# Delta rule on TensorE: where the modulation tiles and the old step's products stand between the levels of a triangular inverse

## The chip, the core and the metric

The kernel runs on one core of a Trainium2 chip. The metric is device time in microseconds (us), the median of three runs: 2932.6 us (2932.4 to 2933.28). A difference under about 0.2% (5.9 us) cannot be told from no change here.

A core has TensorE (matmuls, written PE in the rows, PEld for its weight loads), VectorE (DVE), ScalarE (ACT), GpSimd (POOL) and SyncE (SP, which here only issues DMAs). Each engine runs its own instructions in order and waits for the others through semaphores. Matmul results land in PSUM, which has 8 banks of 512 columns of float32.

## The reference, cut to what matters

The program is one block with a bidirectional gated delta rule and a mixture of experts, then two transformer layers. The change touches only the delta rule of the first block and the modulation product that is computed beside it:

```python
mod = silu(c) @ w_mod + b_mod          # [6 * 1024]; the second network has another of these
# per head (4), per direction (2), in chunks of 64 tokens; 256 context tokens, then 512
lmat = strict_lower((k * beta) @ k.T * decay)
tinv = inverse(eye + lmat)
u, w = tinv @ (v * beta), tinv @ (k * beta * exp(gc))
intra = q @ k.T * decay
def step(s, chunk):                    # in order over the chunks
    v_new = u_i - w_i @ s
    o     = qd_i @ s + a_i @ v_new
    s     = s * gl_i + kd_i.T @ v_new
```

Everything is float32.

## The kernel before, in words

**Tile steps.** The 768 tokens are six tiles of 128 tokens, each two chunks of 64. `delta_pe`, `delta_act` and `delta_dve` write out the programs of TensorE, ScalarE and VectorE for s = -1 to 5. In the round of s, the "new" tile s + 1 is prepared (its triangular inverse is built) while the "old" tile s goes through its two state updates n = 0 and n = 1. Tiles 0 and 1 are context and give no output; for tiles 2 to 5 `with_out` holds. Below, "step k" is the stretch that prepares tile k and ends with its `keys_pe` (line 974); it holds the updates of tile k - 1.

**The inverse.** The 64 by 64 triangle of each head and direction is inverted by block doubling. Level 0 is a mask. For levels l = 1 to 5 and directions d = 0 and 1, `first_pe` (line 947, 16 small products for each direction, bank `TB + d`) is masked by VectorE in `first_dve` (line 1168), `second_pe` (line 964, bank `UB + d`) takes that, and `second_dve` subtracts (line 1175) and transposes (line 1178), after which the next level's `first_pe` can start. Each level so goes twice from TensorE to VectorE and back. `keys_pe` follows level 5.

**The old tile's updates.** `value_pe(s, n)` (lines 984, 994, and 1005 for output) fills bank `VB`, ScalarE copies it (line 1091), `state_pe(s, n)` (lines 1015 and 1022) makes the state's increment and the output. On VectorE `decay_dve` (1187) scales the state, `state_dve` (1192) adds the increment, `out_dve` (1204 or 1207) takes the output, and `query_dve` (1162) scales queries for the tile being prepared.

**The modulation tiles.** `later` is a `RowModulation`: twenty tiles of 512 columns of the two modulation matrices (2 MB each). SyncE loads them into two slots (line 201); the load of tile n + 2 waits until the product of tile n is done. The product of a tile is 64 small matmuls (line 212: weights of one column, 128 moving columns), its row is copied and stored by ScalarE (lines 223 and 225). Before the change a tile stands in front of `second_pe` of direction 0, at levels 1 to 4 in steps 0 and 1 and at levels 2 to 4 in steps 2 to 5, and uses bank `TB`, which `first_pe` of the next level also uses.

**Around it.** Ahead of level 1 of step 0 four groups of transposes for another branch run (`cfturn_pe`, line 76), copied by ScalarE (line 1269). `cf_root_act` (lines 1279 and 1281, with two table loads) stands behind `keys_act` of step 0. When the twentieth tile's product is done, SyncE loads the two halves of `w_out`; `heads_pe` (line 369 there) waits for both. The mixture of experts begins behind a barrier that closes this part, at 576.8 us.

Of the kernel before, what the change touches and what calls it, by code (L numbers as in the profile page):

```python
# [17 lines left out]
NT = T // P  # L18
# [161 lines left out]
class RowModulation:  # L180
# [22 lines left out]
    def pe(self, bank):  # L203

        n, pe, depth, width = self.product.n, self.nc.tensor, len(self.slots), self.COLS // self.GROUPS
        w, cond = self.slots[n % depth], self.parts[n][1]
        pe.wait_ge(self.loaded[n % depth].sem, 16 * (n // depth + 1))
        if n >= 1:
            pe.wait_ge(self.copied.sem, n)
        for k in range(KD):  # L210
            for g in range(self.GROUPS):
                mm = pe.matmul(bank[32 * g:32 * g + 1, 0:width], cond[:, k:k + 1], w[:, k, g * width:(g + 1) * width],
                               start=k == 0, stop=k == KD - 1)
        mm.then_inc(self.product.sem, self.product.up())
# [70 lines left out]
def mixers(nc, X, x_in, c, ctx_in, c_ctx, w_mod, b_mod, g_mix, w_in, w_out, conv_w, a_log, dt_bias, norm_g,  # L285
           cf_w, cf_b, cf_ln_g, cf_ln_b, c_2, mod_w_2, mod_later, consts):
    pe_, act_, dve_, pool_ = nc.tensor, nc.scalar, nc.vector, nc.gpsimd
    with Scope(nc) as ctx:
# [242 lines left out]
        def later_levels(s):  # L531
            return (1, 2, 3, 4) if s < 2 else (2, 3, 4)
# [398 lines left out]
        def first_pe(s, l, d):  # L931

            if l == 1:
                pe_.wait_ge(lt_r.sem, s + 1)
                pe_.wait_ge(m_ev.sem, 2 * s + d + 1)
                if d == 0:
                    if with_out(s):
                        pe_.wait_ge(intra_r.sem, s - NCT + 1)
                    else:
                        pe_.wait_ge(r_relu.sem, 8 * (s + 1))  # L940
            else:
                pe_.wait_ge(up_ev[d].sem, (INV - 1) * s + l - 1)
            if d == 0:
                pe_.wait_ge(later.copied.sem, later.product.n)
            for h in range(4):
                for c in range(2):
                    mm = pe_.matmul(PS[rows(c), TB + d, sq64(0, h)], lt[rows(c), sq64(d, h)], m_of(s, d)[rows(c), sq64(0, h)], start=True, stop=True)
            mm.then_inc(t1_mm[d].sem, t1_mm[d].up())

        def second_pe(s, l, d):  # L950
# [7 lines left out]
            if d == 0 and l in later_levels(s):  # L958
                later.pe(PS[:, TB, :])
# [66 lines left out]
        def delta_pe():  # L1026
# [4 lines left out]
            for s in range(-1, NTA):  # L1031
# [3 lines left out]
                if s < 0:  # L1035
                    cfturn_pe()
                    pe_.wait_ge(cfturn.copied.sem, NT)
# [4 lines left out]
                if not new:  # L1042
                    pe_.wait_ge(cf_silu.sem, NT)
                    for k in (4, 5):
                        heads_turn_pe(k)
                if old:
# [4 lines left out]
                if new:  # L1051
                    for d in range(2):
                        first_pe(s + 1, 1, d)
                if old:
                    value_pe(s, 1)
                if new:
                    for d in range(2):
                        second_pe(s + 1, 1, d)
                    for d in range(2):
                        first_pe(s + 1, 2, d)  # L1060
                if old:
                    state_pe(s, 1)
                if new:
                    for d in range(2):
# [38 lines left out]
        def delta_act():  # L1103
            for s in range(-1, NTA):
# [5 lines left out]
                if old:  # L1110
                    value_act(s, 0)
                if s < 0:
                    cf_square_act()
                if not new:
# [4 lines left out]
                if new:  # L1119
                    for _ in later_levels(s + 1)[:-2]:  # L1120
                        later.act(PS[:, TB, :])
                    scaled_keys_act(s + 1, kg, egc, kg_r)
                    later.act(PS[:, TB, :])
                    scaled_keys_act(s + 1, kd[(s + 1) % 2], ekd, kd_r)
                    later.act(PS[:, TB, :])
# [3 lines left out]
                    if s < 0:  # L1129
                        cf_root_act()  # L1130
# [78 lines left out]
        def delta_dve():  # L1209
            dve_.wait_ge(ld_const.sem, 16)  # L1210
            dve_.memset(ST[:, :], 0.0).then_inc(s_zero.sem, s_zero.up())
            for s in range(-1, NTA):
# [9 lines left out]
                if old:  # L1222
                    state_dve(s, 0)
                    if with_out(s):
                        out_dve(s, 0)
                    if s < LAST:
                        decay_dve(s, 1)
                    else:
                        head_sums_dve((1, 2))
                if new:  # L1230
                    for d in range(2):
                        first_dve(s + 1, 1, d)
                    if with_out(s + 1):
                        query_dve(s + 1)
                    for d in range(2):
                        second_dve(s + 1, 1, d)
                    for d in range(2):
                        first_dve(s + 1, 2, d)
                if old:
                    if s < LAST:  # L1240
                        state_dve(s, 1)
                    if with_out(s):
                        out_dve(s, 1)
                if new:
                    for d in range(2):
                        second_dve(s + 1, 2, d)
                    for l in range(3, INV):
                        for d in range(2):
                            first_dve(s + 1, l, d)
                        for d in range(2):  # L1250
                            second_dve(s + 1, l, d)
                if 0 <= s < NT:
# [7 lines left out]
        def cfturn_pe():  # L1260
            pe_.wait_ge(cf_conv.sem, 4)
            pe_.wait_ge(z_ev.sem, NT)
            for t in range(NT):
# [3264 lines left out]
```

## Time and profile before

| | us |
|---|---|
| median of three runs | 2932.6 |
| the profiled execution | 2939.04 |
| its span, first to last instruction | 2937.2 |
| TensorE busy, of the span | 2702.5 |
| VectorE busy | 1341.7 |
| ScalarE busy | 672.8 |
| delta rule, steps 0 to 5 (270.3 to 502.4) | 232.1 |
| heads stage begins (line 369) | 515.5 |

The times of the parts are those of one profiled execution. "Busy" of TensorE counts a matmul from its start to a modelled end, so that small matmuls in a row overlap and their starts tell more than their sum. A row of the timeline merges instructions of one kind: start, length to the last end, and in brackets how long the engine had been idle and what ended that. The table of windows gives for each stretch the length and, for each engine, busy time and number of instructions; then TensorE's granted clock as a share of 2.4 GHz, the busy share of the DMA engines, and GB/s. "issue" is a wait that the profile puts down to no instruction: a load that had not landed, or instructions that had not come.

### The profile page before, as it was taken

To read this page: it belongs to the slowest core of one execution; us is meant where nothing else is said; L and a number is where in the kernel's file an instruction comes from. 1 tells how busy PE (TensorE), PEld (TensorE's weight loads), DVE (VectorE), ACT (ScalarE), POOL (GpSimd) and SP (SyncE) were. 2 spreads that over 40 slices of the span, in tenths; PEclk is the share of its full clock that TensorE was granted. 3 is DMA by queue.
4 is the path that set the end of the run, shared out by engine and by line. 5 is a ranking of instruction groups with operands and counts; after the bars stand their busy time and mean duration, and the time that the engine had idled before them with its cause. 6 is when DMAs were issued, how large, how long until landed. Compare 5 with 4: busy or idle time off the path is not lost.

```text
span 2937.2 us, 38706 instructions
## 1 busy us (share of the span) xinstructions
PE 2702.5 (92%) x15523; PEld 1743.2 (59%) x15523; DVE 1341.7 (46%) x2785; ACT 672.8 (23%) x1531; POOL 246.7 (8%) x369
## 2 busy tenths in 40 slices
PE   5999888899888898959999999999999999999998
PEld 3545777464333333424466568888844665688887
DVE  2635566452111111164845567754448455433443
ACT  2134233111111111122332433310022324333000
POOL 0000000001111111111110011100012100000000
PEclk9999999999999999979999999999999999999999
DMA  6103545167999999652101035532230110222320
GB/s 237 58 30 127 191 174 189 33 258 303 416 406 411 405 401 407 233 238 110 44 30 66 32 129 208 212 123 86 83 113 26 48 58 29 71 92 91 113 86 29
DMA packets 146807, 469.76 MB, mean 160 GB/s; under 512 B 15389, under 2 KB 28731, under 8 KB 120519
## 3 DMA queue, kind: packets, MB, share of 16 engines
q1 hardware_dynamic: 126468, 416.19, 37.1%
q0 software_dynamic: 18912, 50.36, 4.6%
q8 instruction: 123, 2.02, 0.3%
q10 hardware_dynamic: 1251, 0.77, 0.1%
q14 instruction: 53, 0.43, 0.0%
HBM read 460.90 MB, written 26.28 MB: 166 GB/s over the span
## 4 chain that ended last, share of the span: by engine, by line
PE 48%; DVE 5%; ACT 1%; issue 1%; POOL 0%; DVEq 0%; ACTq 0%; POOLq 0%
PE ps_l L2636 41%; PE ps_l L3158 2%; PE ps_l L76 1%; PE ps_l L3366 1%; DVE pT_notsel_l L3135 1%; PE ps_l L3824 1%; DVE small_l L3133 1%; DVE small_l L3484 1%; PE ps_l L3194 1%; DVE pT_notsel_l L3125 0%; PE ps_l L3240 0%; PE ps_l L159 0%; PE ps_l L3104 0%; PE ps_l L2820 0%; PE ps_l L3465 0%
## 5 line engine op out<-in xcount | busy, mean ns | idle before, releaser
L2129 PE MATMUL ps_m<-w_m,gatheredT_m 128*64 128x512 f32 (+1 forms) x816 | 305.3, 637 | 48.2 <-issue 46.4
L2636 PE MATMUL ps_l<-ring_l,hT_l 128*128 128x256 f32 (+3 forms) x960 | 313.2, 469 | 0.0
L2636 PE MATMUL ps_l<-early,hT_l 128*128 128x512 f32 (+1 forms) x576 | 260.6, 591 | 6.6 <-ACT hT_l L2827 3.0
L2636 PEld LDWEIGHTS ps_l<-ring_l,hT_l 128*128 128x128 f32 x960 | 174.6, 190 | 104.1 <-issue 83.2
L2129 PEld LDWEIGHTS ps_m<-w_m,gatheredT_m 128*64 128x64 f32 (+1 forms) x816 | 107.9, 164 | 180.6 <-issue 178.8
L2247 DVE TENSOR_TENSOR silu_m<-silu_m,ps_m 128x256 f32<-128x256 f32 x42 | 17.7, 421 | 360.1 <-ACT silu_m L2199 359.9
L2636 PE MATMUL ps_l<-hT_l,ring_l 128*128 128x256 f32 (+1 forms) x704 | 179.9, 405 | 0.9 <-ACT arena_l L3715 0.9
L369 PE MATMUL ps_a<-arena_a,ring_a 128*128 128x512 f32 (+2 forms) x496 | 169.9, 519 | 0.9 <-DVE arena_a L516 0.9
L2636 PE MATMUL ps_l<-ring_l,arena_l 128*128 128x256 f32 x768 | 169.1, 379 | 0.7 <-ACT arena_l L168 0.7
L2636 PEld LDWEIGHTS ps_l<-early,hT_l 128*128 128x128 f32 x576 | 104.9, 193 | 106.5 <-issue 96.4
L2636 PEld LDWEIGHTS ps_l<-ring_l,arena_l 128*128 128x128 f32 x768 | 145.8, 190 | 21.4 <-ACT arena_l L168 1.6
L2636 PEld LDWEIGHTS ps_l<-hT_l,ring_l 128*128 128x128 f32 x704 | 134.7, 193 | 30.1 <-issue 11.1
L2153 PE MATMUL ps_m<-w_m,aT_m 128*64 128x512 f32 (+1 forms) x408 | 145.3, 597 | 1.1 <-DVE aT_m L2257 1.1
L369 PEld LDWEIGHTS ps_a<-arena_a,ring_a 128*128 128x128 f32 (+1 forms) x496 | 87.3, 182 | 83.8 <-issue 77.9
L2129 PE MATMUL ps_m<-hT_m,gatheredT_m 128*64 128x512 f32 (+1 forms) x240 | 119.2, 655 | 16.2 <-issue 16.2
L2636 PE MATMUL ps_l<-consts_l,work_l 128*128 128x256 f32 x512 | 122.1, 381 | 2.5 <-DVE consts_l L3754 2.5
L2199 ACT ACTIVATE silu_m<-ps_m 128x256 f32<-128x256 f32 x42 | 16.1, 383 | 438.5 <-PE ps_m L2129 438.5
L2636 PEld LDWEIGHTS ps_l<-consts_l,work_l 128*128 128x128 f32 x512 | 96.3, 190 | 24.5 <-issue 11.9
L2636 PE MATMUL ps_l<-hT_l,early 128*128 128x256 f32 x384 | 89.0, 380 | 0.9 <-ACT ropework_l L3715 0.9
L130 DVE SCALAR_TENSOR_TENSOR gla_l<-pT_notsel_l,small_l,gla_l 128x256 f32<-128x256 f32 x168 | 81.5, 485 | 6.0
L2253 DVE COPY rows_io_m<-ps_m 128x512 f32<-128x512 f32 x42 | 29.0, 691 | 120.4 <-PE ps_m L2153 120.4
L2153 PEld LDWEIGHTS ps_m<-w_m,aT_m 128*64 128x64 f32 (+1 forms) x408 | 47.9, 153 | 55.4 <-issue 53.3
(620 smaller groups left out, 4209.1 us busy)
## 6 DMA issues: line engine op xcount, KB each, us to landing
w_m<-in_exp_w_gate SPq DMA_DIRECT2D x51, 1024.0 KB
w_m<-in_exp_w_up SPq DMA_DIRECT2D x51, 1024.0 KB
w_m<-in_exp_w_down SPq DMA_DIRECT2D x51, 1024.0 KB, 12.7
ring_l<-in_mlp_w SPq DMA_DIRECT2D x22, 2048.0 KB, 7.8
ring_a<-in_mod_w SPq DMA_DIRECT2D x12, 2048.0 KB, 9.3
pT_notsel_l<-in_mod_w POOLq DMA_DIRECT2D x24, 1024.0 KB, 5.6
early<-in_mlp_w SPq DMA_DIRECT2D x10, 2048.0 KB, 7.9
ring_a<-in_w_mod SPq DMA_DIRECT2D x9, 2048.0 KB, 9.0
```

Of the source, the lines that this page charges most:

```text
L76: mm = self.nc.tensor.transpose(self.banks[n % len(self.banks)][0:src.shape[1], bank_cols], src, self.ident[0:src.shape[0], 0:src.shape[0]])
L130: dve.scalar_tensor_tensor(out, w[:, k, :], cond[:, k:k + 1], out, ALU.mult, ALU.add).then_inc(signal.sem, signal.up())
L369: mm = pe_.matmul(out, lhsT, rhs, start=start, stop=stop)
L2129: mm = pe_.matmul(PS[h * rows:(h + 1) * rows, 2, :], hg[s % 2][:, k, h * rows:(h + 1) * rows], gu_w[w][:, k, :, :], start=k == 0, stop=k = ...
L2153: mm = pe_.matmul(PS[h * rows:(h + 1) * rows, 4 + half, :], AT[:, at:at + rows], dn_w[w][:, k, half * 512:(half + 1) * 512], start=k == 0, ...
L2636: mm = pe_.matmul(out, lhsT, rhs, start=start, stop=stop, **group)
L3133: dve_.max(top, nb[:, i, 0:s]).then_inc(own_v.sem, own_v.up())
L3135: dve_.match_replace(nb[:, i, 0:s], top, nb[:, i, 0:s], TAKEN).then_inc(own_v.sem, own_v.up())
L3158: mm = pe_.matmul(PS[:, 6, h * 64:(h + 1) * 64], src[:, j, h, :], proj[:, j, c:c + 64], start=j == 0, stop=j == i)
L3194: pe_.matmul(PS[:, h, 0:s], TB[o:o + 64, h // 2, i * P:(i + 1) * P], TB[o:o + 64, 6, 0:s], start=True, stop=True).then_inc(at_mm.sem, at_m ...
L3366: mm = pe_.matmul(PS[:, 2 * (n % 2) + h % 2, 0:P], a_, b_, start=True, stop=True, tile_position=(32 * h, 0))
L3484: dve_.tensor_reduce(mx[:, b:b + 2], PS[:, b:b + 2, 0:s], AX.X, ALU.max).then_inc(own_v.sem, own_v.up())
```

## The change

- The product of a modulation tile is cut in two halves of 32 matmuls (`pe(bank, half)`), and stands behind `second_pe` of a level instead of in front of it. Steps 2 to 4 have a tile at levels 3, 4 and 5, step 5 at levels 2, 3 and 4. Step 1 has one ahead of the first state product and at levels 3, 4 and 5. Step 0 has one between the transposes, one spread over levels 1 and 2, one over levels 3 and 4, and one at level 5. It stays at twenty tiles.
- Its bank is `OB` for tiles 0 and 1 and `VB` after them; `first_pe` no longer waits for the copy of a tile, `value_pe` does.
- `value_pe(s, 1)` stands behind the second products of level 1 (it stood in front of them), `state_pe(s, 1)` behind those of level 2.
- VectorE follows: the first output copy stands between the two passes of level 1, `decay_dve` behind level 1, `state_dve` behind level 2, the second output copy behind level 3, `query_dve` behind level 4. In the last round its order stays.
- ScalarE: `cf_root_act` moves from behind `keys_act` of step 0 to directly behind `cf_square_act`; the tile copies follow their tiles.

```diff
-    def pe(self, bank):
+    def pe(self, bank, half):
...
-        pe.wait_ge(self.loaded[n % depth].sem, 16 * (n // depth + 1))
-        if n >= 1:
-            pe.wait_ge(self.copied.sem, n)
-        for k in range(KD):
+        if half == 0:
+            pe.wait_ge(self.loaded[n % depth].sem, 16 * (n // depth + 1))
+            if n >= 1:
+                pe.wait_ge(self.copied.sem, n)
+        for k in range(half * KD // 2, (half + 1) * KD // 2):
...
-        def later_levels(s):
-            return (1, 2, 3, 4) if s < 2 else (2, 3, 4)
+        BEFORE_STATE = 0
+        def later_halves(s):
+            if s == 0:
+                return {BEFORE_STATE: (0, 1), 1: (0,), 2: (1,), 3: (0,), 4: (1,), 5: (0, 1)}
+            if s == 1:
+                return {BEFORE_STATE: (0, 1), 3: (0, 1), 4: (0, 1), 5: (0, 1)}
+            return {l: (0, 1) for l in ((3, 4, 5) if s < NTA - 1 else (2, 3, 4))}
...
+        def later_bank(s):
+            return PS[:, OB if s < NCT else VB, :]
+        def later_pe(s, at):
+            for half in later_halves(s).get(at, ()):
+                later.pe(later_bank(s), half)
         def value_pe(s, n):
             if vn_mm.n:
                 pe_.wait_ge(vn_ev.sem, vn_mm.n)
+            pe_.wait_ge(later.copied.sem, later.product.n)
...
                 if new:
-                    for d in range(2):
-                        second_pe(s + 1, 2, d)
-                    for l in range(3, INV):
+                    for l in range(1, INV):
                         for d in range(2):
                             first_pe(s + 1, l, d)
                         for d in range(2):
                             second_pe(s + 1, l, d)
+                        if old and l == 1:
+                            value_pe(s, 1)
+                        if old and l == 2:
+                            state_pe(s, 1)
+                        later_pe(s + 1, l)
                     keys_pe(s + 1)
...
                 if s < 0:
                     cf_square_act()
+                    cf_root_act()
...
                 if new:
-                    for l in range(3, INV):
+                    for l in range(1, INV):
                         for d in range(2):
                             first_dve(s + 1, l, d)
+                        if old and l == 1 and with_out(s):
+                            out_dve(s, 0)
                         for d in range(2):
                             second_dve(s + 1, l, d)
+                        if old and l == 1:
+                            decay_dve(s, 1)
+                        if old and l == 2:
+                            state_dve(s, 1)
+                        if old and l == 3 and with_out(s):
+                            out_dve(s, 1)
+                        if l == 4 and with_out(s + 1):
+                            query_dve(s + 1)
```

TensorE, before, from level 1 to the first product of level 3 in steps 4 and 5 (L947 is the first product, L964 the second, L984 to L1005 the value product, L1015 and L1022 the state product, L212 a modulation tile):

```order
L947 MATMUL ps_a<-arena_a 64x64 x16
L984 MATMUL ps_a<-tok_a,arena_a 64x128 x8
L994 MATMUL ps_a<-states_a,arena_a 64x128 x8
L1005 MATMUL ps_a<-states_a,arena_a 64x128 x8
L964 MATMUL ps_a<-arena_a 64x64 x16
L947 MATMUL ps_a<-arena_a 64x64 x16
L1015 MATMUL ps_a<-arena_a 128x128 x8
L1022 MATMUL ps_a<-arena_a 64x128 x8
L212 MATMUL ps_a<-ring_a,cond_a 1x128 x32
L964 MATMUL ps_a<-arena_a 64x64 x16
L947 MATMUL ps_a<-arena_a 64x64 x16
```

The same stretch of TensorE in the changed kernel, up to the first tile (L957 is now the first product, L972 the second, L1000 to L1021 the value, L1031 and L1038 the state product, L213 a tile):

```order
L957 MATMUL ps_a<-arena_a 64x64 x16
L972 MATMUL ps_a<-arena_a 64x64 x16
L1000 MATMUL ps_a<-tok_a,arena_a 64x128 x8
L1010 MATMUL ps_a<-states_a,arena_a 64x128 x8
L1021 MATMUL ps_a<-states_a,arena_a 64x128 x8
L957 MATMUL ps_a<-arena_a 64x64 x16
L972 MATMUL ps_a<-arena_a 64x64 x16
L1031 MATMUL ps_a<-arena_a 128x128 x8
L1038 MATMUL ps_a<-arena_a 64x128 x8
L957 MATMUL ps_a<-arena_a 64x64 x16
L972 MATMUL ps_a<-arena_a 64x64 x16
L213 MATMUL ps_a<-ring_a,cond_a 1x128 x32
```

The value, state and tile products stood between a first and a second product; now they stand between a second product and the next level's first, and the first tile has moved from level 2 to level 3.

TensorE at the start of step 0 in the changed kernel, from the transposes (L76) to level 2; before, both groups of transposes stood together and a whole tile of x32 stood between L947 and L964 at each of levels 1 to 4:

```order
L76 MATMUL ps_a<-consts_a,cf_o_a 128x128 x8
L213 MATMUL ps_a<-ring_a,cond_a 1x128 x32
L76 MATMUL ps_a<-consts_a,cf_o_a 128x128 x8
L957 MATMUL ps_a<-arena_a 64x64 x16
L972 MATMUL ps_a<-arena_a 64x64 x16
L213 MATMUL ps_a<-ring_a,cond_a 1x128 x16
L957 MATMUL ps_a<-arena_a 64x64 x16
L972 MATMUL ps_a<-arena_a 64x64 x16
L213 MATMUL ps_a<-ring_a,cond_a 1x128 x16
```

A tile has gone ahead of level 1, and each of levels 1 and 2 has half a tile behind its second product.

VectorE of the changed kernel in step 3, from the first output copy on (L1220 output copy, L1188 subtraction, L1191 transpose, L1200 scaling of the state, L1181 mask of a first product, L1205 state sum):

```order
L1220 COPY cf_o_a<-ps_a 64x512 x2
L1188 TENSOR_TENSOR arena_a<-arena_a,ps_a 128x256
L1191 STREAM_TRANSPOSE arena_a<-arena_a 128x256
L1188 TENSOR_TENSOR arena_a<-arena_a,ps_a 128x256
L1191 STREAM_TRANSPOSE arena_a<-arena_a 128x256
L1200 TENSOR_TENSOR arena_a<-states_a,chunk_decay_a 128x1024
L1181 TENSOR_TENSOR arena_a<-ps_a,consts_a 128x256 x2
L1188 TENSOR_TENSOR arena_a<-arena_a,ps_a 128x256
L1191 STREAM_TRANSPOSE arena_a<-arena_a 128x256
L1188 TENSOR_TENSOR arena_a<-arena_a,ps_a 128x256
L1191 STREAM_TRANSPOSE arena_a<-arena_a 128x256
L1205 TENSOR_TENSOR states_a<-arena_a,ps_a 128x1024
```

The long operations (output, scaling, state sum) stood ahead of a level's masks or between them and the subtractions; now each stands behind the work of a level, the output copy alone stands in front of subtractions.

## Rows read from the trace of the kernel before

**Rows 1.** Windows, one per tile step (0 to 5); columns as explained above
```profile
270.32:305.70 35.38, 26.85 (x657) 21.97 (x657) 15.28 (x36) 15.61 (x47) 0.00 (x0) 0.90 0.77 272
305.70:347.09 41.39, 32.38 (x768) 28.11 (x769) 19.58 (x39) 13.35 (x36) 0.00 (x0) 0.92 0.59 206
347.09:382.59 35.50, 31.17 (x752) 27.20 (x753) 23.88 (x46) 11.40 (x33) 0.00 (x0) 1.00 0.49 175
382.59:424.46 41.87, 35.62 (x816) 31.91 (x817) 26.71 (x50) 11.40 (x33) 0.00 (x0) 0.96 0.50 179
424.46:462.98 38.52, 34.69 (x817) 30.72 (x817) 26.70 (x50) 11.40 (x33) 0.00 (x0) 1.00 0.38 137
462.98:502.38 39.40, 34.74 (x817) 30.80 (x817) 26.67 (x50) 14.87 (x38) 0.00 (x0) 1.00 0.34 117
```

**Rows 2.** Timeline, TensorE, step 4: start us, us, engine line operation, idle
```profile
436.40 1.10 PE L947 MATMUL ps_a<-arena_a 64*64 64x64 f32 x32
437.33 1.04 PE L984 MATMUL ps_a<-tok_a,arena_a 64*64 64x128 f32 x16
...
440.20 1.15 PE L964 MATMUL ps_a<-arena_a 64*64 64x64 f32 x32
...
443.88 1.16 PE L1015 MATMUL ps_a<-arena_a 64*128 64x128 f32 x16
...
445.99 1.93 PE L212 MATMUL ps_a<-ring_a,cond_a 128*1 128x128 f32 x64
447.85 1.15 PE L964 MATMUL ps_a<-arena_a 64*64 64x64 f32 x32
...
459.69 1.47 PE L947 MATMUL ps_a<-arena_a 64*64 64x64 f32 x32 [0.54 <-DVE arena_a L1178]
460.98 1.38 PE L964 MATMUL ps_a<-arena_a 64*64 64x64 f32 x32
462.98 2.00 PE L974 MATMUL ps_a<-arena_a 64*128 64x64 f32 x32 [0.62 <-DVE arena_a L1175]
```

**Rows 3.** Groups by line, VectorE, 270 to 516 us: busy, mean ns, idle
```profile
L1168 DVE TENSOR_TENSOR arena_a<-ps_a,consts_a 128x256 f32<-128x256 f32 x60 | 25.0, 423 | 13.6 <-PE ps_a L947 13.4
L1175 DVE TENSOR_TENSOR arena_a<-arena_a,ps_a 128x256 f32<-128x256 f32 x60 | 24.3, 405 | 47.2 <-PE ps_a L964 47.0
L1178 DVE STREAM_TRANSPOSE arena_a<-arena_a 128x256 f32<-128x256 f32 x48 | 21.4, 445 | 1.7
L1187 DVE TENSOR_TENSOR arena_a<-states_a,chunk_decay_a 128x1024 f32<-128x1024 f32 x11 | 13.4, 1221 | 0.2
```

**Rows 4.** DMA issues, one tile load each, issued at 448.0, 406.1 and 377.7 us
```profile
ring_a<-in_mod_w SPq DMA_DIRECT2D x1, 2048.0 KB, 7.8
...
ring_a<-in_mod_w SPq DMA_DIRECT2D x1, 2048.0 KB, 9.1
...
ring_a<-in_mod_w SPq DMA_DIRECT2D x1, 2048.0 KB, 11.7
```

**Rows 5.** Timeline, ScalarE, step 1
```profile
308.78 1.28 ACT L1279 ACT_TABLE_LOAD   x1
```

**Rows 6.** Timeline, TensorE, first product of step 0, and state product in step 1
```profile
278.80 1.97 PE L947 MATMUL ps_a<-arena_a 64*64 64x64 f32 x32 [1.73 <-ACT cf_o_a L1269]
...
314.63 1.55 PE L1015 MATMUL ps_a<-squares_a,arena_a 64*128 64x128 f32 x16 [2.72 <-ACT squares_a L1091]
```

**Rows 7.** Windows: three stretches of TensorE's clock
```profile
277.90:284.70 6.80, 5.90 (x108) 4.47 (x109) 1.88 (x6) 3.21 (x9) 0.00 (x0) 0.51 0.01 4
315.40:322.20 6.80, 5.41 (x66) 4.81 (x66) 5.29 (x9) 0.00 (x0) 0.00 (x0) 0.51 0.00 0
338.60:342.00 3.40, 1.74 (x65) 1.60 (x64) 0.42 (x1) 0.27 (x1) 0.00 (x0) 1.00 1.03 379
```

**Rows 8.** Timeline, TensorE, last modulation tile of step 1
```profile
340.26 1.93 PE L212 MATMUL ps_a<-ring_a,cond_a 128*1 128x128 f32 x64 [1.66 <-issue]
```

**Rows 9.** DMA issues, the second load of w_out, issued at 498 us
```profile
ring_a<-in_w_out SPq DMA_DIRECT2D x1, 2048.0 KB, 13.5
```

More of the change, by code:

```diff
@@ L213, in pe @@
                                start=k == 0, stop=k == KD - 1)
-        mm.then_inc(self.product.sem, self.product.up())
+        if half == 1:
+            mm.then_inc(self.product.sem, self.product.up())
     def act(self, bank):
@@ L529, in mixers, with later_copies @@
                            [SQ[:, 1088 + r * P:1088 + (r + 1) * P] for r in range(2)], mod_later)
-        def later_levels(s):
-            return (1, 2, 3, 4) if s < 2 else (2, 3, 4)
+        BEFORE_STATE = 0
[5 more added lines that the diff above has]
+            return {l: (0, 1) for l in ((3, 4, 5) if s < NTA - 1 else (2, 3, 4))}
+        def later_copies(s):
+            return sum(halves.count(1) for at, halves in later_halves(s).items() if at != BEFORE_STATE)
         p_mm, p_ev, cb_zero, conv, conv_silu = sig("p_mm"), sig("p_ev"), sig("cb_zero"), sig("conv"), sig("conv_silu")
@@ L1035, in delta_pe @@
                 if s < 0:
-                    cfturn_pe()
+                    cfturn_pe((0, 1))
+                    later_pe(s + 1, BEFORE_STATE)
+                    cfturn_pe((2, 3))
                     pe_.wait_ge(cfturn.copied.sem, NT)
@@ L1045, in delta_pe @@
                         heads_turn_pe(k)
+                if old and new:
+                    later_pe(s + 1, BEFORE_STATE)
                 if old:
@@ L1111, in delta_act @@
                     value_act(s, 0)
+                if new and BEFORE_STATE in later_halves(s + 1):
+                    later.act(later_bank(s + 1))
                 if s < 0:
                     cf_square_act()
+                    cf_root_act()
                 if not new:
@@ L1119, in delta_act @@
                 if new:
-                    for _ in later_levels(s + 1)[:-2]:
-                        later.act(PS[:, TB, :])
                     scaled_keys_act(s + 1, kg, egc, kg_r)
-                    later.act(PS[:, TB, :])
+                    later.act(later_bank(s + 1))
                     scaled_keys_act(s + 1, kd[(s + 1) % 2], ekd, kd_r)
-                    later.act(PS[:, TB, :])
+                    for _ in range(later_copies(s + 1) - 1):
+                        later.act(later_bank(s + 1))
                     if s == LAST - 1:
@@ L1258, in mixers, with cfturn_pe @@
         mu, vr = S[:, 448:452], S[:, 452:456]
-        def cfturn_pe():
+        def cfturn_pe(tiles_):
             pe_.wait_ge(cf_conv.sem, 4)
             pe_.wait_ge(z_ev.sem, NT)
-            for t in range(NT):
+            for t in tiles_:
                 cfturn.pe([(cc[:, cch, t * P:(t + 1) * P], slice(cch * P, (cch + 1) * P)) for cch in range(4)])
```

42 lines of the change are left out of this document (4 added, 38 removed).

## The prediction

> **What bounds the kernel now.** I read the stretch in which the change works, 270 to 502 us of a 2937 us span, first by windows of one tile step each. TensorE is busy 32 to 36 of about 40 us, VectorE 20 to 27, ScalarE 11 to 16 [rows 1]. The reader is to see that no engine is full: the steps are a chain that goes back and forth between TensorE and VectorE, and what counts is who stands in whose way. The timeline of step 4, a step with little disturbance, shows it. Level 5 has no tile: its first product starts at 459.69, its second at 460.98, `keys_pe` at 462.98. Half a microsecond ahead of the first and 0.62 us ahead of `keys_pe` TensorE is idle and waits for VectorE; at level 2 a tile (445.99 to 447.85, 1.86 us) stands ahead of the second product [rows 2]. By groups, VectorE needs 0.42 us for a mask, 0.41 for a subtraction, 0.45 for a transpose [rows 3] and waits 47 us in all for second products, since the tile holds them up. So before the change a tile covers only the short mask; the longer stretch, subtraction and transpose, is paid in idle time, and so is the tile.
>
> The second limit is the load. Each tile is 2 MB in one of two slots, and the slot of the third tile of a step is free only when the first is used up. Such a load takes 7.8 us with nothing in front of it, 9.1 in another step, 11.7 queued behind another [rows 4].
>
> **One level.** At level 5 today first and second product together take 2.60 us (1.29 to the second product's start, 1.3 for it) [rows 2], of which 0.3 is the wait of direction 1 for its transpose. Behind a tile or an old product both transposes are done and the two directions run without a gap, so I put the pair at 2.35 us (2.3 if nothing waits). With a whole tile a level then takes 2.35 + 1.86 = 4.2 us, with half a tile 3.3. VectorE's subtraction, transpose and again both, about 1.7 us by [rows 3], lie beside the tile. Before, a level with a tile took 1.1 + 1.86 + 1.1 and 0.54 idle, with 0.3 of transposes between the directions: 4.9 us.
>
> **Step 4, part by part.** `keys_pe` to the first product of level 1 is 436.40 - 424.46 = 11.94 us and is not changed [rows 1, 2]. From there, counted from 0: level 1 until 2.35; the value product 440.20 - 437.33 = 2.87, until 5.22; level 2, where the state's scaling of 1.22 us [rows 3] stands ahead of the masks and costs 0.2, until 7.77; the state product 445.99 - 443.88 = 2.11, until 9.88; level 3 until 12.23, tile until 14.09; level 4 with 0.2 for the output copy in front of the masks, 16.64, tile until 18.50; level 5 until 20.85. There the third tile is not ready. Its slot came free at 14.09, the load is issued 0.13 us later and takes 8.5 us (my value between 7.8 and 9.1, the middle): 22.7. With the tile, 24.6. The step takes 36.5 us instead of 38.52, a gain of 2.0 (2.7 with 7.8, 1.4 with 9.1). The wait of 1.9 us is new: before, the two levels between the tiles covered the load almost to the point.
>
> **The other steps, in the same way.** Step 5 has its tiles at levels 2 to 4 and the same wait at level 4: 37.1 instead of 39.40, gain 2.3. Step 3 is built as step 4 but took 41.87, 3.35 more than step 4 with the same instructions [rows 1]; it comes to 36.5, gain 5.4. Step 2 has shorter value and state products: 34.2 instead of 35.50, gain 1.3. Step 1: before, two table loads of 1.28 us each with their operations stand in ScalarE's order ahead of the copy that the state product needs (308.78) [rows 5], and TensorE is idle 2.72 us, until 314.63 [rows 6]. With these two behind the squares in step 0, where ScalarE has slack, `keys_pe`, setup and value product take 6.0 us, the tile that now stands there 1.9, beside ScalarE's chain, the state product 1.1: the first level begins at 9.1 instead of 11.9. Two levels without a tile, three with one, a value and a state product and the wait of about 1.9 us for the load give 33.0 instead of 41.39, gain 8.4. Step 0: the first product of level 1 stays at 278.80, since ScalarE's copies of the transposes release it [rows 6]. Four levels of 3.3 and a copy that holds one tile back by 0.35 are 13.5, level 5 with its tile 4.2: 296.5 instead of 305.70, gain 9.2. But in this stretch the clock was at 1.2 GHz from 277.9 to 284.7 (granted 0.51) [rows 7]; TensorE was idle ahead of it, and the tile between the transposes now fills part of that. If the clock falls all the same, half of what TensorE does in the stretch comes back, 5.90 / 2 = 2.9 us. I take 7.8, between 6.3 and 9.2. The stretch after 315.4, also at 1.2 GHz [rows 7], followed the 2.72 us of idle time, which goes; at worst 2.7 us come back.
>
> The sum is 7.8 + 8.4 + 1.3 + 5.4 + 2.0 + 2.3 = 27.2 us. Step 3's 3.35 us and 0.9 of step 5 over step 4 are stalls of the instruction or load supply that nothing in the change removes; I let half of them return, 2.1. That leaves 25.1 us. The added waits: the third tile delays `keys_pe` (priced above); `value_pe` waits for a tile's copy, 0.3 us on ScalarE, under the 1.9 us of `keys_pe`: nothing, at most 0.4 a step if that cover were gone. The tiles' new banks are free where they stand: nothing. SyncE's queue holds only the loads.
>
> Four more changes between a tile's array shape (128*1) and the level's (64*64) come from the halves of step 0; the tile's 64 matmuls and the second product behind them run on at 1.86 us without a gap [rows 2], so I price them at 0. The Trainium skill, TensorEngine Tiling (Array Packing), section Tiling Modes, says that a change of the tiling mode drains the array. By it each of the four would cost about one matmul's length, an estimate of 1 us in all; the row speaks for nothing.
>
> The profiled execution took 2939.04 us, 6.4 more than the median of 2932.6; the gain is taken off the median, where it is the same 0.9%. 2932.6 - 25.1 = 2907.5, rounded to 2907. What follows the barrier cannot give it back, because the experts' loads are issued only behind it.
>
> **The rivals.**
> 1. The waits for the third tile let the clock fall. Five steps get a wait of 1.9 us in a stretch of small matmuls. If each is followed by 6.8 us at half speed as in [rows 7], 5 x 2.9 = 14.5 us come back: 2922. For it: the two falls of [rows 7] followed idle TensorE. Against it: step 1 had a wait of 1.66 us for a load [rows 8], and the window around it shows a clock of 1.00 [rows 7]. The Trainium skill, TensorE: Matmul & The Clock Gate, section Loop structure matters more than you think, calls a DMA wait between groups of matmuls what makes the array go cold; by that rule the time would be this one.
> 2. The loads land early and the clock stays up: 0.7 us a step more, 1.4 in step 0, no stalls back (2.1), levels of 2.3: 2907.5 - 8 = 2899. For it: 7.8 has been seen with an idle queue [rows 4].
> 3. Slower. The loads of the third tiles, on which five steps now hang, land late. Each us beyond 8.5 costs 5 us and a little at step 0. To lose the 25.1 us they must take 8.5 + 25.1 / 5.5 = 13.1 us, and about 14.1 to be visibly slower (2939). The most seen in a ring load with one ahead is 11.7 [rows 4], the second load of `w_out` took 13.5 [rows 9]; but after the change the third tile's load has nothing ahead of it. 2939 and more.
> 4. It doesn't do what it says, because the heads stage waits for `w_out`: the second load is issued 0.5 us behind the last tile and takes 13.5 [rows 9], landing 14.1 behind it. The heads stage now begins about 16 us behind the last tile (level 5, `keys_pe`, two updates), before 18. The cover shrinks to 2 us; it would have to be gone by 20 us more for no change.
>
> **How the numbers follow.** Forecast with stalls and one or two short falls of the clock, 2901 to 2914: 0.62. Rival 1 whole or in part, 2914 to 2926: 0.17. Rival 2, below 2901: 0.14. No visible change (2927 to 2938; under 0.2%, 5.9 us, this measurement tells nothing): 0.04, rivals 1 and 4 together. Rival 3: 0.03. The range goes from 2898 to 2919: it holds the forecast, most of rival 2 and the lower half of rival 1. Faster 0.93, same 0.04, slower 0.03.
>
> **What would show it.** Steps of 36 to 37 us in 3 to 5 and 33 in step 1 (starts of `keys_pe`); a tile right behind each second product and no idle time ahead of levels 3 to 5; VectorE's wait for second products well under 47 us; at level 5 (4 in step 5) idle TensorE ahead of the tile, 1.2 to 2.5 us, ended by the load; step 0 ended by 296 to 300. The prediction is wrong if that wait is over 4 us, if the clock falls after each of them, or if the masks wait behind the moved state work by more than 1 us a level.

## The result: 0.54% faster, two thirds of the forecast gain

| | before | after |
|---|---|---|
| time, median of 20 runs each, us | 2936.34 (2932.34 to 2943.61) | 2918.62 (2908.21 to 2935.25) |
| ratio of the times | 1 | 0.9946, interval 0.9932 to 0.9959 |
| profiled execution, us | 2939.04 | 2926.64 |
| its span, us | 2937.2 | 2924.8 |
| stage: first setup product to the heads stage, us | 245.17 | 227.61 |
| of it steps 0 to 5, us | 232.1 | 214.5 |

The ratio is a gain of 15.9 us, the medians differ by 17.7, and the stage is 17.6 shorter; I had forecast 25.1 for it. The time lies at the upper edge of the range, 11.6 us above the forecast; 3.7 of these come from the starting point, since the kernel before has a median of 2936.34 over twenty executions where it had 2932.6 over three. The whole times scatter by several microseconds from one execution to the next (2908 to 2935 after the change). What lies behind the stage took 2421.7 us in the profiled execution before and 2429.0 after, 2418 to 2432 in the experiments below that can be compared; why is open. So I compare stages, and use whole times as a check.

The windows of one tile step each, of the kernel after (start to end us, length, busy us of TensorE, its weight loads, VectorE, ScalarE, GpSimd, granted clock, DMA share, GB/s), answer to [rows 1]:

```profile
268.22:296.98 28.76, 23.71 (x658) 20.20 (x657) 16.28 (x36) 18.10 (x50) 0.00 (x0) 1.00 0.77 268
296.98:335.88 38.90, 33.22 (x772) 29.05 (x769) 21.20 (x41) 10.49 (x32) 0.00 (x0) 0.88 0.65 230
335.88:369.65 33.77, 30.48 (x756) 27.38 (x752) 23.58 (x45) 11.30 (x33) 0.00 (x0) 0.98 0.47 165
369.65:407.03 37.38, 34.24 (x821) 30.69 (x817) 26.54 (x49) 11.29 (x33) 0.00 (x0) 0.98 0.54 194
407.03:445.09 38.06, 35.25 (x821) 31.65 (x817) 26.54 (x49) 11.29 (x33) 0.00 (x0) 0.95 0.48 170
445.09:482.72 37.63, 34.43 (x820) 31.04 (x817) 23.71 (x46) 13.58 (x37) 0.00 (x0) 0.99 0.40 134
```

The engines do the same work in less time, and the clock is no better than before: step 1 is at 0.88 where it was at 0.92, step 4 at 0.95 where it was at 1.00. Step 4 in TensorE's timeline (start us, us, engine, line, operation, idle before and who ended it) answers to [rows 2]:

```profile
431.28 1.93 PE L213 MATMUL ps_a<-ring_a,cond_a 128*1 128x128 f32 x64
433.14 1.15 PE L957 MATMUL ps_a<-arena_a 64*64 64x64 f32 x32
434.44 1.15 PE L972 MATMUL ps_a<-arena_a 64*64 64x64 f32 x32 [0.15 <-DVE arena_a L1181]
435.52 1.93 PE L213 MATMUL ps_a<-ring_a,cond_a 128*1 128x128 f32 x64
437.38 1.15 PE L957 MATMUL ps_a<-arena_a 64*64 64x64 f32 x32
438.59 1.15 PE L972 MATMUL ps_a<-arena_a 64*64 64x64 f32 x32
442.14 3.02 PE L213 MATMUL ps_a<-ring_a,cond_a 128*1 128x128 f32 x64 [2.40 <-DMA ring_a<-in_mod_w]
```

The reader is to see three things. Tiles and products stand with no gap over 0.15 us: a level with a tile takes 435.52 - 431.28 = 4.24 us (4.9 before). The one new wait stands where it was expected, ahead of the third tile, and it is 2.40 us instead of the assumed 1.9. And the tile behind that wait takes 3.02 us instead of 1.93: its clock fell. Windows of such stretches (same columns), which answer to [rows 7]:

```profile
299.50:306.30 6.80, 6.80 (x96) 6.45 (x96) 0.27 (x1) 3.40 (x10) 0.00 (x0) 0.50 0.77 288
402.00:405.40 3.40, 1.07 (x40) 0.98 (x44) 3.04 (x5) 0.00 (x0) 0.00 (x0) 0.98 1.03 352
405.40:408.80 3.40, 3.40 (x50) 2.71 (x44) 0.00 (x0) 0.28 (x1) 0.00 (x0) 0.52 0.92 314
442.90:446.30 3.40, 3.40 (x56) 2.60 (x50) 0.35 (x1) 0.28 (x1) 0.00 (x0) 0.51 0.93 339
```

With one more of 3.4 us from 333.7, TensorE works at 1.2 GHz for 17.0 us in all, as long as before (6.8 from 278.0, 6.8 from 315.5, 3.4 from 421.3). The window ahead of 405.40 shows what went before: 1.07 us of work in 3.40, since the third tile waited 2.73 us.

TensorE's waits by line, 268 to 496 us (us in total, times, longest), sum this up:

```profile
PE ps_a L213 <- DMA ring_a<-in_mod_w: 9.0, 4, 2.7
PE ps_a L213 <- DMA ring_a<-in_w_mod: 2.8, 1, 2.8
...
PE ps_a L972 <- issue: 1.6, 1, 1.6
PE ps_a L982 <- issue: 1.5, 1, 1.5
PE ps_a L957 <- issue: 0.9, 1, 0.9
```

The five waits for loads cost 11.8 us (2.75, 1.72, 2.73, 2.40, 2.19 in steps 1 to 5). "Issue" is idle time for which no engine and no load is named; three of these stand in steps 0 and 1:

```profile
283.33 0.91 PE L972 MATMUL ps_a<-arena_a 64*64 64x64 f32 x23 [1.62 <-issue]
...
293.08 0.91 PE L957 MATMUL ps_a<-arena_a 64*64 64x64 f32 x23 [0.88 <-issue]
...
299.09 2.55 PE L982 MATMUL ps_a<-arena_a 64*128 64x64 f32 x24 [1.45 <-issue]
```

They stand in the middle of a group of 32 matmuls (9 and then 23, 8 and then 24), where no matmul waits for a semaphore: TensorE lacks its next instructions. The trace shows these arriving, as packets of 16 KB on a DMA queue called "instruction" (39 of them from 268 to 510 us). In front of each stall such a packet ends, and TensorE goes on 1.3 to 1.6 us later:

| packet starts, us | ends | TensorE goes on | between |
|---|---|---|---|
| 280.88 | 281.99 | 283.33 | 1.34 |
| 290.50 | 291.53 | 293.08 | 1.55 |
| 296.70 | 297.77 | 299.09 | 1.32 |

It is so for all 45 stalls in the middle of a group in this run and the seven experiments that keep the new order (1.22 to 1.67 us). The trace doesn't say which engine a packet is for; but one comes every 6 us or so, and by chance about one stall in thirteen would fit. Behind the last of the three comes the fall of 6.8 us, which is why step 1 takes 38.90.

VectorE's wait for second products, by groups (busy, mean ns, idle), answers to [rows 3]:

```profile
L1188 DVE TENSOR_TENSOR arena_a<-arena_a,ps_a 128x256 f32<-128x256 f32 x60 | 24.4, 406 | 11.9 <-PE ps_a L972 11.5
```

It fell from 47.2 to 11.9 us, while the operation still takes 0.41 us: the reordering did what it was to do.

### The profile page after: what moved, and what is told of

It is laid out like the page before. It is cut to its first block, busy times and chain, and to the rows that moved or that the text cites. A ratio compares the mean times of both kernels' runs of the same rounds, so it can differ in the third digit from the quotient of the medians.

```text
span 2924.8 us, 38689 instructions
## 1 busy us (share of the span) xinstructions
PE 2700.2 (92%) x15523; PEld 1741.1 (60%) x15523; DVE 1341.0 (46%) x2785; ACT 672.9 (23%) x1531; POOL 247.3 (8%) x369
## 4 chain that ended last, share of the span: by engine, by line
PE 46%; DVE 6%; ACT 1%; issue 1%; SPq 0%; POOL 0%; DMA 0%; DVEq 0%; ACTq 0%; POOLq 0%
PE ps_l L2641 40%; PE ps_l L3163 2%; DVE pT_notsel_l L3140 1%; DVE small_l L3138 1%; PE ps_l L76 1%; PE ps_l L3371 1%; DVE pT_notsel_l L3130 1%; PE ps_l L3829 1%; DVE small_l L3489 1%; PE ps_l L3199 0%; PE ps_l L3245 0%; PE ps_l L159 0%; PE ps_l L3470 0%; DVE work_l L3503 0%; PE ps_l L3378 0%
## 5 line engine op out<-in xcount | busy, mean ns | idle before, releaser
L2252 DVE TENSOR_TENSOR silu_m<-silu_m,ps_m 128x256 f32<-128x256 f32 x42 | 17.7, 421 | 368.1 <-ACT silu_m L2204 367.9
L2641 PEld LDWEIGHTS ps_l<-hT_l,ring_l 128*128 128x128 f32 x704 | 134.7, 193 | 30.1 <-issue 11.1
L2641 PEld LDWEIGHTS ps_l<-consts_l,work_l 128*128 128x128 f32 x512 | 96.3, 190 | 24.5 <-issue 11.9
```

The lines of the kernel that those rows point to most:

```text
L2641: mm = pe_.matmul(out, lhsT, rhs, start=start, stop=stop, **group)
```

## The experiments

All edits are to the changed kernel unless said otherwise. A stage is that of the profiled execution of the run named; the stages of two executions of the same kernel differed by 1.7 us, which is the measure for small differences.

**The changed kernel once more.** No edit.

> The changed kernel once more, beside the others. Stage time means: from the first setup product of step 0 to the heads stage; before 245.2 us, changed 227.6 us in the traces at hand. Theory A (the stage gains 17.6 us, the rest of the program only scatters): stage 225 to 230, whole time 15 to 20 us below before. Theory B (the parts behind the stage give some of it back, as 7 us in the one trace): stage the same, whole time only 10 to 13 us below before.

Measured: 0.9936 (0.9921 to 0.9952), 18.8 us of the whole time, stage 225.9 us, as theory A has it. The load waits are the same in kind (2.70, 1.55, 2.71, 2.07, 2.11, together 11.1), and so is the half-speed time, 17.0 us, but not its place: 3.4 us from 279.8, 10.2 from 402.7, 3.4 from 477.8. Two of the three issue stalls return at the same matmul as before, to the instruction:

```profile
294.71 0.91 PE L957 MATMUL ps_a<-arena_a 64*64 64x64 f32 x23 [0.88 <-issue]
...
300.72 1.55 PE L982 MATMUL ps_a<-arena_a 64*128 64x64 f32 x24 [1.45 <-issue]
```

Here no fall of the clock follows the second, and step 1 takes 35.3 us. The third, of 1.62 us, is missing: the fall from 279.8 had held TensorE up ahead of it, and the packet, which ends at 283.75, came almost in time. Two small ones are new (0.31 and 0.28 us). So the load waits and most of the stalls are a property of the program; whether a fall follows one of them is not, and a fall can take a stall away.

**Half of each load.**

```
-        eng.dma_start(self.slots[r], self.parts[n][0])...
+        eng.dma_start(self.slots[r][:, 0:KD // 2, :], self.parts[n][0][:, 0:KD // 2, :])...
```

It leaves out half of each modulation tile's load. The modulation values are then others, what lies behind the stage takes some 100 us longer (I suppose since the experts get other tokens; not shown), and the whole time (2994.58 us) can't be compared; the stage can.

> Loads only the first 1 MB of each 2 MB modulation tile (the product then uses old data in the other half; leaves out half of the load). Theory A (the wait for the third tile of a step, 2.2 to 2.8 us in five steps, the falls of the clock behind it and the stalls of the instruction supply, 4 us in steps 0 and 1, all come from the load): stage 227.6 - 12 - 2 - 2 = about 212, no idle ahead of a tile. Theory B (the wait matters, but clock and stalls are of their own): stage 215 to 216. Theory C (a new wait takes its place): stage over 220.

Measured: stage 204.2 us, under the 212 of theory A, because more clock came back than the 2 us put down for it. Windows of steps 0, 1 and 5:

```profile
270.11:295.96 25.85, 23.30 (x657) 20.00 (x656) 16.28 (x36) 17.98 (x50) 0.00 (x0) 1.00 0.50 161
295.96:327.10 31.14, 29.03 (x772) 25.62 (x769) 19.47 (x40) 10.49 (x32) 0.00 (x0) 1.00 0.43 138
...
426.07:461.19 35.12, 33.90 (x820) 30.55 (x817) 25.42 (x48) 13.59 (x37) 0.00 (x0) 1.00 0.26 82
```

The clock is at 1.00 throughout, no tile waits for a load, and two issue stalls are left (0.63 and 0.23). With the loads at half their size all three losses go together: load waits, falls of the clock and most of the stalls. The stall that is left at the end of step 0 stands at the same matmul as the one of 1.45 us, and its packet starts 1.00 us ahead of `keys_pe` instead of 0.28. The packet of the 1.62 us stall tells more: it starts 12.66 us into the stage, in the second execution 12.70, with half loads 9.54, each time as the weights' transfers run out (the DMA share falls from about 1 to under 0.1 there), while TensorE was at its 270th, 232nd and 176th matmul of the stage. So it hung on the weights rather than on how far TensorE had got. This is what the chain of the new order takes with nothing in its way, and the base of the account below.

**Tiles spread so that the third load has time.**

```
             if s == 1:
-                return {BEFORE_STATE: (0, 1), 3: (0, 1), 4: (0, 1), 5: (0, 1)}
-            return {l: (0, 1) for l in ((3, 4, 5) if s < NTA - 1 else (2, 3, 4))}
+                return {BEFORE_STATE: (0, 1), 2: (0, 1), 3: (0,), 4: (1,), 5: (0, 1)}
+            return {2: (0, 1), 3: (0,), 4: (1,), 5: (0, 1)}
```

> Steps 1 to 5 have their tiles at level 2 (whole), level 3 (first half), level 4 (second half), level 5 (whole), so that the slot of the last tile comes free 9 us ahead of its use. Theory A (the load wait is what was mis-sized and can be covered by order alone): no wait over 0.5 us ahead of the last tile, steps 2 to 5 at 34 to 35 us, stage 216 to 218, with w_out landing about 1 us late for the heads stage. Theory B (the load wait is replaced by idle time at the levels with half a tile): stage 222 or more.

Measured: 0.9931 (0.9916 to 0.9947), stage 227.2 us, theory B. No load wait is left, and yet the stage is as long as after the change. TensorE's waits say why:

```profile
PE ps_a L982 <- issue: 6.3, 4, 2.2
...
PE ps_a L957 <- issue: 3.5, 3, 1.7
PE ps_a L1010 <- ACT arena_a L1108: 2.4, 1, 2.4
PE ps_a L957 <- DVE arena_a L1161: 1.8, 1, 1.8
PE ps_a L972 <- issue: 1.6, 1, 1.6
```

The issue stalls rise from 4 to 11.6 us, and the clock is down for 10.2 us (6.8 from 334.3, 3.4 from 484.5). Masks hold second products up for 6.0 us (2.6 in the changed kernel). The last tile at level 5 of step 5 also puts its copy into ScalarE's way, ahead of the copy of the keys (L1108), and the value product on the states (L1010) waits 2.38 us for that: from the end of step 5 to the heads stage it takes 16.8 us instead of 13.1. Spreading moves the loss, it doesn't remove it.

**Only the tiles moved; the old step's products back where they were.** In `delta_pe` value and state products of direction 1 stand again between first and second product of levels 1 and 2, and `delta_dve` has its order of before.

```
-                        for d in range(2):
-                            second_pe(s + 1, l, d)
                         if old and l == 1:
                             value_pe(s, 1)
                         if old and l == 2:
                             state_pe(s, 1)
+                        for d in range(2):
+                            second_pe(s + 1, l, d)
...
```

> Undoes one part of the changed kernel: the old step's value and state products and VectorE's order stand as before the change, the tiles stay behind the second products. Theory A (both moves pay; levels 1 and 2 then pay about 1.1 and 0.5 us of idle time): stage 234 to 236. Theory B (the tile placement does it all): stage 228.

Measured: 0.9993 (0.9979 to 1.0007), stage 235.0 us, within theory A, 10.2 us of it at half speed. The first products of levels 2 and 3 wait for VectorE's transpose again, nine times, 10.4 us in all (us in total, times, longest; then two of them in step 3's timeline):

```profile
PE ps_a L957 <- DVE arena_a L1191: 10.4, 9, 1.7
```
```profile
385.32 1.47 PE L957 MATMUL ps_a<-arena_a 64*64 64x64 f32 x32 [1.13 <-DVE arena_a L1191]
...
391.52 1.47 PE L957 MATMUL ps_a<-arena_a 64*64 64x64 f32 x32 [1.69 <-DVE arena_a L1191]
```

**Only the products moved; the tiles back ahead of the second products.** In `second_pe`, for d == 0 and the levels of before (`first_pe` of direction 0 then waits for a tile's copy again):

```
+            if d == 0 and l in ((1, 2, 3, 4) if s < 2 else (2, 3, 4)):
+                for half in range(2):
+                    later.pe(PS[:, TB, :], half)
```

> Undoes the other part of the changed kernel: the tiles stand in front of the second products as before the change, the value and state products, VectorE's order and the root stay as changed. Stage time (before 245.2, changed 226 to 228). Theory A (levels with a tile pay 0.5 us of idle time and the late transpose again, and the tile's load has two levels and a tile to land in, as before): stage 236 to 240, tile waits as before the change (under 1.7 us). Theory B (without the new waits for the load the old place is as good): stage 228 to 231.

Measured: 0.9982 (0.9969 to 0.9994), stage 238.9 us, 20.5 us of it at half speed (6.8 from 277.1, 3.4 from 314.7, 10.2 from 413.7), and within theory A. The longest wait that can be for a load is 1.35 us. TensorE's waits:

```profile
PE ps_a L959 <- DVE arena_a L1190: 7.5, 14, 0.5
...
PE ps_a L213 <- DVE arena_a L1180: 3.6, 5, 1.1
PE ps_a L959 <- issue: 3.2, 4, 1.4
```

The stage gains 10.2 us from the tiles alone and 6.3 from the products alone, 16.5 together, against 17.6 and 19.3 for both. But the clock was at half speed for 10.2 us in the one execution and 20.5 in the other, against 17.0; with half of the difference counted back, the gains are 6.8 and 8.0, 14.8 together. So these are two parts of similar size that give most of the whole; that the raw numbers add up so well is in part luck. In whole time each alone gives 2 and 5 us, where the change gives 15.9.

**The roots back in step 1.** `cf_root_act()` again behind `keys_act(s + 1)`.

```
-                    cf_root_act()
...
+                    if s < 0:
+                        cf_root_act()      # behind keys_act
```

> The changed kernel with ScalarE's root and its two table loads again behind the keys' copy of step 0. Theory A (they held the state product of step 1 back by 2.7 us): step 1 longer by 2 to 3 us, stage 229 to 230. Theory B (the modulation tile that now stands there covers them): under 1 us.

Measured: 0.9949 (0.9930 to 0.9968), stage 228.3 us. Step 1 takes 40.35 us against 38.90, both with the fall of 6.8 us from 299.5. The 1.5 us is between the two expectations and not above what two executions differ by; its visible part is a wait of 0.91 us ahead of a first product at 312.08, with no instruction packet near it. This part of the change is worth little at most.

**A third slot for the tiles.** A part of the array of `cf_o`, free once the squares are taken (the first load into it waits for that), and the arrays of the gates' bias become a third slot, so that a load can start one tile's product sooner (n - 2 products done instead of n - 1).

```
-        if n >= len(self.slots):
-            eng.wait_ge(self.product.sem, n - len(self.slots) + 1)
+        if n == 2 or n > 3:
+            eng.wait_ge(self.product.sem, 1 if n == 2 else n - 2)
...
+                           + [[part(CFO, 4 * T, 4 * 512, a=4), part(GBT, 0, 4 * 512, a=4)]],
```

> The changed kernel with a third slot for the tiles' loads, in two pieces of memory that are free in this stage; every tile is loaded in full. Theory A (the load, not the order, holds the stage back: with half the load it took 204.2): no wait for a tile's load, no fall of the clock behind one; stage 204 plus the 4 to 6 us of stalls in the instruction supply that the loads cause, 208 to 212; whole time 15 us below the changed kernel, about 2903. Theory B (as in the spread order: what the load wait took, stalls of the instructions and clock falls take instead): stage 222 or more. Theory C (w_out lands late for the heads stage): tail over 13.1 us.

Measured: 2906.21 us (2902.90 to 2917.34), ratio 0.9899 (0.9879 to 0.9919), stage 215.7 us, 3.7 us over theory A and far under B. It beats both kernels: its interval doesn't meet that of the change (0.9932 to 0.9959). Windows of its steps 0, 1 and 5:

```profile
269.95:300.50 30.55, 23.98 (x658) 20.16 (x657) 16.29 (x36) 18.06 (x50) 0.00 (x0) 1.00 0.93 325
300.50:334.21 33.71, 30.50 (x772) 27.03 (x768) 19.47 (x40) 10.49 (x32) 0.00 (x0) 0.95 0.62 216
...
437.99:472.55 34.56, 33.55 (x820) 30.33 (x817) 25.43 (x48) 13.57 (x37) 0.00 (x0) 1.00 0.36 126
```

No load wait, one fall of 3.4 us (from 304.4), and step 5 is 34.6 us as with half loads (35.1). Step 0, where the loads now stand closer (325 GB/s against 268), became 1.8 us longer: what is left is issue stalls, 9.4 us in eight of them, of which the largest groups are

```profile
PE ps_a L995 <- issue: 3.0, 3, 1.7
PE ps_a L225 <- issue: 2.8, 2, 1.4
```

(L995 is the first product of `keys_pe` there, L225 the tile's).

**The same third slot in the kernel before.** The same edit.

> The kernel before the change with the same third slot. Theory A (before the change the order, not the load, was the limit; the load cost it 1.1 and 1.7 us and some stalls): stage 239 to 243. Theory B (the load was the limit already): stage under 230.

Measured: 0.9986 (0.9974 to 0.9997), stage 243.2 us, as theory A has it but for 0.2 us. The half-speed time is 17.0 us as before. So the third slot is worth 2.0 us in the old order and 10 to 12 in the new one; before, as the prediction had it, the levels between the tiles covered the load almost to the point.

**Work in the place of the wait.** Ahead of the last tile of steps 1 to 5, 64 matmuls whose result nothing reads:

```
+        def filler_pe(s):
+            pe_.wait_ge(later.copied.sem, later.product.n)
+            for _ in range(2): ...
+                pe_.matmul(later_bank(s)[rows(c), sq64(d, h)], kk, kk, start=True, stop=True)
```

> The changed kernel with 64 more small products (2.2 us, of constant keys, into the bank that the tile then overwrites) ahead of the last tile of steps 1 to 5, where TensorE otherwise waits 1.7 to 2.8 us for that tile's load. They change no result and take the place of the wait. Theory A (the falls of the clock come from the idle time of that wait, and each us of a fall costs half a us): no fall behind a load wait, one or none in steps 0 and 1, stage 227.6 - 4 to 6 = 221 to 224 although TensorE does more. Theory B (the falls don't hang on the wait): falls as before, stage 226 to 231.

Measured: 0.9946 (0.9931 to 0.9962), stage 235.0 us, longer than either theory has it. The load waits shrink to 0.6 us and half-speed time to 6.8 us. But the issue stalls grow from 3 or 4 to 15.5 us, and both falls that are left follow one of them, not a load (timeline, then windows around 414.8):

```profile
407.54 1.50 PE L997 MATMUL ps_a<-kT_qT_a 128*64 128x64 f32 x43 [1.27 <-issue]
...
414.00 0.99 PE L982 MATMUL ps_a<-arena_a 64*128 64x64 f32 x12 [1.84 <-issue]
```
```profile
411.40:414.80 3.40, 1.56 (x26) 1.42 (x24) 0.00 (x0) 0.00 (x0) 0.00 (x0) 0.98 0.94 286
414.80:418.20 3.40, 3.40 (x62) 3.17 (x62) 0.00 (x0) 2.29 (x8) 0.00 (x0) 0.52 1.01 379
```

So a fall can follow idle time that no load ended. The added work took the place of the load waits, about 11 us for 11 us; beyond that it brought 11.6 us more of stalls and saved only 5.1 at the clock.

## Why the prediction was right and wrong

The direction and the mechanism were right; the gain was forecast at 25.1 us and was 17.6. The stage with half loads gives the base for an account by terms:

| term of the stage | forecast, us | measured, us | off by |
|---|---|---|---|
| chain of the new order, nothing in its way | 207.1 | 204.2 | -2.9 |
| waits for third tiles | 9.5 | 11.8 | +2.3 |
| half-speed clock (half of its time) | 1.4 | 8.5 | +7.1 |
| issue stalls | 2.1 | 3.1 | +1.0 |
| sum | 220.1 | 227.6 | +7.5 |

The forecast of the chain is 245.2 - 25.1 less the other three terms; the measured stalls are 3.95 less the 0.86 that stand with half loads too; 17.0 us at half speed are counted as 8.5. The same account holds for the second execution: 204.2 + 11.1 + 8.5 + 2.1 = 225.9, as measured. For the third slot it gives 214.4 of 215.7.

- **Levels.** 3.3 us with half a tile and 4.2 with a whole one: measured 287.44 - 284.17 = 3.27 (from one half's start to the next in step 0) and 4.24. Right; the chain as a whole was even 2.9 us shorter.
- **Masks behind the moved state work.** 0.15 us at level 4 of step 4, under the 0.2 allowed; in steps 1 and 2 three waits of 0.65 us for masks, 2.6 us in the whole stage. Far under the 1 us a level named. Right.
- **Halves of step 0 at no cost.** The rows of step 0 run on without a gap:

```profile
286.37 1.15 PE L972 MATMUL ps_a<-arena_a 64*64 64x64 f32 x32
287.44 1.05 PE L213 MATMUL ps_a<-ring_a,cond_a 128*1 128x128 f32 x32
288.43 1.15 PE L957 MATMUL ps_a<-arena_a 64*64 64x64 f32 x32
```

  A half takes 0.99 us from start to start, half of a whole tile 0.93; four such halves cost 0.2 us. The Trainium skill, TensorEngine Tiling (Array Packing), section Tiling Modes, has the array drained at such a change; if it is, less than 0.1 us of it shows here.
- **Waits for the third tile.** 1.9 us assumed, 2.36 in the mean. The load issued at 433.27 lands 8.8 us later instead of 8.5, and the next one behind it 10.3 later. The price of one load was about right, and the place as well. No wait was over the 4 us named.
- **The clock.** This is the step that failed: the term for the clock, put at 1.4 us, measured 8.5. The prediction let one fall return at half weight ("I take 7.8, between 6.3 and 9.2") and took the one after 315.4 as gone. A third one it did not see: step 3's 3.35 us [rows 1, clock 0.96] were put down to stalls, but the trace of before has 3.4 us at half speed from 421.1 there, beside stalls of 0.63 and 1.38. The falls did leave the places that they had, 278.0, 315.5 and 421.3, and came at new ones: 17.0 us at half speed before, 17.0 after, 17.0 once more in the second execution. That the three sums are equal is no rule: the experiments had 0 to 20.5. The change made of idle time that was in part spread over many small waits (24 for a transpose, 14.8 us) five waits of 1.5 to 2.8 us, and a fall followed three of them in one execution and two in the other. Rival 1 was thus right in part. It asked for falls of 6.8 us behind all five, and had 2922; two or three of 3.4 to 10.2 us came.
- **Why I argued it away.** I leaned on one wait of 1.66 us without a fall [rows 8]. Of the new waits in two executions those of 1.55, 1.72, 2.07, 2.19 and 2.70 us had none either, those of 2.11, 2.40, 2.71, 2.73 and 2.75 had one. With the root back, one of 2.89 us had none. One row of 1.66 us was too little to say so for waits of 2.4 us. The Trainium skill, TensorE: Matmul & The Clock Gate, section Loop structure matters more than you think, has a long DMA wait between every matmul make the array go cold; the prediction left out the word long. Here it happened behind 5 of 10 waits for loads, and also behind stalls that were none (299.5 after the change, 414.8 with the filler).
- **Issue stalls.** I let half of those of before return, as if they came by chance. Mostly they do not: two of three stand at the same matmul in both executions, and the third was missing where the clock had fallen ahead of it.
- **Step by step.** Gains 6.6, 2.5, 1.7, 4.5, 0.5 and 1.8 us against 7.8, 8.4, 1.3, 5.4, 2.0 and 2.3. The largest miss is step 1 (5.9 us), where a stall of 1.45 us is followed by 6.8 us at half speed; in the execution without that fall it was 35.3.
- **The heads stage** came 13.11 us behind step 5, as before. Rival 4 did not happen; its second load of `w_out` was covered. Rival 3 did not either: no third tile's load came near 13 us.
- **Rival 2** (2899) is nearly what the third slot gives, 2906: with the load wait gone, most of the clock comes back with it.

The stalls are waits for the next 16 KB of instructions; that much the traces show. They shrink with the amount of weights in flight (0.9 us with half loads) and grow with the loads' density (9.4 with three slots) and with the number of instructions (15.5 with 320 more matmuls). For one stall the packet starts just as the weights' transfers run out, in three runs. Open is what holds the other packets back, since the trace doesn't show when they were asked for, and I made no run that changes them alone. Open too is what decides whether a fall follows a wait of some two microseconds, and why the parts of the change taken alone gave less in whole time than in their stages.

## What to carry to other kernels

Filling idle slots with a tile's work also shortens the time that the next tile's load has to land: after a reordering, count from the freed slot to the next use again, and add a slot if it comes short (here 2.0 us in the old order, 10 to 12 in the new). Price a wait in a stretch of small matmuls at more than its length: of the waits for loads of 1.5 to 2.8 us here half were followed by a fall of the clock that costs 1.7 us or more. Do not take idle time that falls together with dense loads as noise: look whether it stands at the same instruction in a second execution, and whether a packet on the instruction queue ends just ahead of it.

## What the runs showed of the hardware

- In this stage TensorE runs out of instructions for up to 1.6 us at a time while 2 MB loads are in flight, in the middle of a group (2.2 us in the experiments), most often at the same instruction in a second execution; with loads of half the size only 0.6 and 0.2 us are left. In all 45 such stalls of the new order a packet of 16 KB on the instruction queue had ended 1.22 to 1.67 us before TensorE went on.
- Falls of the clock to 1.2 GHz lasted 3.4, 6.8 or 10.2 us and came in or behind idle time: waits of 1.3 to 2.9 us in all runs but for one fall, which came with two of 0.70 and 0.95 us close together (314.7, tiles back). Waits of the same length passed without a fall (2.70 us in the second execution, 2.89 with the root back). The same program had its falls at other places in another execution.
- A 2 MB load took 8.8 us with the next one issued 4.2 us behind it, and that one 10.3.
